# Zero products in the mixer of a two-layer block: seven, one and one at the start of each layer in place of eight spread over it

## The reference

```python
for l in range(DEPTH):
    x = layer_norm(ALPHA * x + 0.5 * swiglu(x, ffn_w1[l, 0], ffn_w2[l, 0]), ...)
    mix = hybrid_mixer(x, w_in[l], ...)
    x = layer_norm(ALPHA * x + mix, ...)
    x = layer_norm(ALPHA * x + 0.5 * swiglu(x, ffn_w1[l, 1], ffn_w2[l, 1]), ...)

def hybrid_mixer(x, ...):
    proj = x @ w_in                                  # 1024 x 7168
    b_gate, c_gate, v, x_r, y_r, g_logits = split(proj)
    y_a = (b_gate * causal_depthwise_conv(c_gate * v, sc_w, 3)) @ w_out_conv
    xc = causal_depthwise_conv(x_r, rc_w, 4) + rc_b
    gates = sigmoid(per-head 256x256 products of xc + rg_b)
    h = rg_lru(xc, gates[0], gates[1], a_param)      # a scan over the tokens
    y_b = (h * gelu(y_r)) @ w_out_rnn
    g_a, g_b = split(sigmoid(g_logits + b_merge))
    return (g_a * y_a + g_b * y_b) @ w_o
```

## Time and profile before

| | |
|---|---|
| median of three runs | 1782.72 us (1781.75 to 1782.98) |
| the profiled execution | 1781.71 us, its span 1780.0 us |
| TensorE products (PE) | 1750.6 us busy, 98% of the span, 10818 products |
| TensorE weight loads (PEld) | 1543.8 us, 87% |
| VectorE (DVE) | 1372.5 us, 77% |
| ScalarE (ACT) | 988.6 us, 56% |
| chain that ended last | PE 81%, DVE 10%, ACT 3% |
| 256-column products of `cols_unit` (L2295 to L2297) | 912 of each line, 254.0 us each |
| mean granted clock of TensorE | 0.997 |

### The profile page before, as it was taken

One profiled execution on the slowest core, in us unless ns is written; L12 is line 12 of the kernel. 1 busy time (PEld: TensorE's weight loads), 2 busy tenths in 40 slices (PEclk: granted clock), 3 DMA queues, 4 the chain that ended last, 5 costly groups with the idle time before them and its releaser, 6 DMA issues.

```text
span 1780.0 us, 27901 instructions
## 1 busy us (share of the span) xinstructions
PE 1750.6 (98%) x10818; PEld 1543.8 (87%) x10818; DVE 1372.5 (77%) x1544; ACT 988.6 (56%) x973; POOL 60.9 (3%) x103
## 2 busy tenths in 40 slices
PE   9999999999999999999999999999999989999998
PEld 8888899998888878888999988888899868777776
DVE  7656886857778875567878667788878888889988
ACT  5555465643544545445656435445544636879984
POOL 2000000000000000000000000000200010000002
PEclk9999999999999999999999999999999999999999
DMA  7555455564577645554555645777454029989994
GB/s 267 202 174 207 173 188 188 190 252 150 198 274 283 260 168 184 191 200 179 177 202 181 246 166 173 280 283 274 139 175 143 24 91 339 385 301 412 426 376 159
DMA packets 58487, 395.21 MB, mean 222 GB/s; under 512 B 7216, under 2 KB 7616, under 8 KB 12816
## 3 DMA queue, kind: packets, MB, share of 16 engines
q1 hardware_dynamic: 48800, 350.31, 53.7%
q0 software_dynamic: 9568, 43.44, 7.2%
q10 hardware_dynamic: 16, 0.01, 0.0%
HBM read 386.37 MB, written 7.36 MB: 221 GB/s over the span
## 4 chain that ended last, share of the span: by engine, by line
PE 81%; DVE 10%; ACT 3%; DVEq 3%; issue 3%; ACTq 0%
PE ps L2304 18%; PE ps L2312 9%; PE ps L2296 8%; PE ps L2297 8%; PE ps L2295 8%; PE ps L2502 3%; PE ps L2501 3%; PE ps L2505 3%; DVE wlo L1844 3%; PE ps L1035 2%; DVE wlo L2810 2%; PE ps L1037 2%; PE ps L1036 2%; PE ps L1099 1%; ACT whi L1344 1%
## 5 line engine op out<-in xcount | busy, mean ns | idle before, releaser
L2810 DVE TENSOR_TENSOR wlo<-raw,whi 128x2048 fp32r<-128x2048 f32 x235 | 536.5, 2289 | 238.4 <-ACT whi L2635 236.4
L2635 ACT ACTIVATE whi<-raw 128x2048 fp32r<-128x2048 f32 x235 | 449.2, 1912 | 375.3 <-PE ps L2505 170.7
L2304 PE MATMUL ps<-xT,whi 128*128 128x512 f32 x1408 | 340.0, 393 | 2.6 <-DVE xT L2829 2.2
L2304 PEld LDWEIGHTS ps<-xT,whi 128*128 128x128 f32 x1408 | 262.4, 188 | 60.4 <-DVE xT L2829 3.0
L2295 PE MATMUL ps<-xT,whi 128*128 128x256 f32 x912 | 254.0, 278 | 0.3 <-DVE wlo L2810 0.3
L2297 PE MATMUL ps<-xT,wlo 128*128 128x256 f32 x912 | 254.0, 279 | 0.0
L2296 PE MATMUL ps<-xT,whi 128*128 128x256 f32 x912 | 254.0, 279 | 0.0
L2312 PEld LDWEIGHTS ps<-xT,wlo 128*128 128x128 f32 x1408 | 174.1, 188 | 7.8
L2312 PE MATMUL ps<-xT,wlo 128*128 128x256 f32 x1408 | 175.5, 277 | 0.0
L2296 PEld LDWEIGHTS ps<-xT,whi 128*128 128x128 f32 x912 | 171.3, 188 | 0.6
L2295 PEld LDWEIGHTS ps<-xT,whi 128*128 128x128 f32 x912 | 171.1, 188 | 0.5 <-DVE wlo L2810 0.5
(11 more groups left out here) (616 smaller groups left out, 3204.0 us busy)
## 6 DMA issues: line engine op xcount, KB each, us to landing
raw<-stream SPq DMA_DIRECT2D x236, 1024.0 KB, 4.9
raw<-experts SPq DMA_DIRECT2D x64, 1024.0 KB, 7.6
mod<-experts SPq DMA_DIRECT2D x32, 1024.0 KB, 7.3
adaraw<-ada POOLq DMA_DIRECT2D x24, 1024.0 KB, 5.1
yd<-lnrow POOLq DMA_DIRECT2D x7, 512.0 KB, 7.8
lnrow<-ln_g POOLq DMA_DIRECT2D x6, 512.0 KB, 4.9
lnrow<-ln_b POOLq DMA_DIRECT2D x6, 512.0 KB, 6.7
yd<-lnrow POOLq DMA_DIRECT2D x10, 256.0 KB, 6.5
```

Of the source, the lines that this page charges most:

```text
L2304: last = nc.tensor.matmul(bank(b), whi[:, slot, c:c + P], xT[:, k].rearrange("p a t -> p (a t)"), start=k == 0, stop=False)
L2635: act_fn(whi[:, slot, :], raw[:, slot, :], ACT.Copy).then_inc(hi_done, 1)
L2810: v.tensor_tensor(wlo[:, slot, :], raw[:, slot, :], whi[:, slot, :].bitcast(F32), ALU.subtract).then_inc(lo_done, 1)
```

## The change

The leads of the second half, of u6 and u11 of the first half, and of the conv and rnn units go. In the first half of each layer u1 gets seven leads in a row, u2 one and u3 one. That is nine leads in a layer, where there were eight.

```diff
-LED_UNITS = (1, 6, 11)
+LED_UNITS = {1: 7, 2: 1, 3: 1}
...
                 weights_ready(rnd, slot)
                 if lead is not None:
-                    nc.tensor.matmul(bank(lead), zero_w[:, :], whi[:, slot, 0:512], start=True, stop=True)
+                    b, count = lead
+                    for _ in range(count):
+                        nc.tensor.matmul(bank(b), zero_w[:, :], whi[:, slot, 0:512], start=True, stop=True)
...
-                                cols_unit(rnd, slot, xThi, xTlo, [bank(b, 0, T), bank(b, T)], b if u in LED_UNITS else None)
+                                cols_unit(rnd, slot, xThi, xTlo, [bank(b, 0, T), bank(b, T)],
+                                          (b, LED_UNITS[u]) if hf == 0 and u in LED_UNITS else None)
...
-                        cols_unit(*at(base, i), yahi, yalo, [bank(q, 0, T), bank(q, T)], q if q == 0 else None)
+                        cols_unit(*at(base, i), yahi, yalo, [bank(q, 0, T), bank(q, T)])
...
-                        cols_unit(*at(base, i), ybhi, yblo, [bank(q, 0, T), bank(q, T)], q if q == 0 else None)
+                        cols_unit(*at(base, i), ybhi, yblo, [bank(q, 0, T), bank(q, T)])
```

## The result

| | before | changed |
|---|---|---|
| median, seven executions each, one comparison | 1782.72 us (1781.75 to 1784.50) | 1789.96 us (1786.30 to 1790.96) |
| the profiled execution | 1781.71 us | 1790.06 us |
| its mean granted clock | 0.997 | 0.995 |

The ratio is 1.0036, 95% interval 1.0025 to 1.0046: slower, by some 7 us, where 9.6 us less were forecast.

The account below looks back on a forecast made before the run. TensorE, never idle, bounds the mixer. Fast units win 10.0 us, leads cost 0.4 us: 9.6 us off the profiled 1781.71 us gives 1772.1 us, plus 1.0 us for the median 1773.1 us; whole range 1771.5 to 1787.7 us.

Parts of the forecast that it names:

- What bounds the mixer: Mixer: TensorE busy throughout (27.20 of 27.20 us), its products are the path; units take 5.440 or 5.653 us, changing at leads.
- The leads' price: Mixer: sixteen leads go (3.8 us), eighteen come (4.2 us), seven in a row costing 1.63 us; net 0.4 us more.
- The place behind seven leads: Ahead of u1: seven leads forget their beginning and leave one slow place; 70 of 74 units fast, 10.0 us won; chance 0.50.
- slow-one: Mixer stream's place one lead after fast: 5.653 us a unit, with two more leads needed to make it fast.
- The seven settle in another place: Ahead of u1: seven end in fast or slow-two, leaving 2 fast units of 74; 4.9 us more, 1787.6 us; chance 0.28.
- No lead comes after, so u3 to the last rnn unit, 35 units a layer, stay fast: Mixer from u3 on: the fast pace lasts without leads, 70 of 74 units fast; 47 units at 0.213 us, 10.0 us won.
- what hides the rest: Mixer: VectorE's splits may come late once u6 to u10 are fast; 20 units stay slow, 4.3 us given back, 1777.4 us.
- 23 of 74: Mixer units from u1 to the last rnn unit that are fast before the change: 14 in layer 0, 9 in layer 1.
- Mere counting: Ahead of u1: seven leads act as one; 36 fast units, 2.8 us won, 0.4 us paid, 1780.3 us; chance 0.19.
- slow-two: Mixer stream's place one lead after slow-one: slow pace, 5.653 us a unit, and the next lead makes fast.
- The pace is not the leads' doing: Mixer: leads do not set the pace, only two more leads count; 0.4 us more, 1783.1 us; chance 0.03.

Follow-up runs that it names:

- the first map: The changed kernel with single leads and groups of 2 to 8 and 16 ahead of every unit of `cols_unit` in both layers; 1813.78 us.

## Why the prediction was wrong

*What bounds the mixer*: right. TensorE has no pause in the changed mixers; the paces are 5.44 and 5.65 us a unit in every run, nothing between but where a unit meets a wait; leads move the place.

*The leads' price*: right. Seven 1.62 us (1.63 forecast, ends 1.58 and 1.82), nine in a layer 2.1 us.

*The place behind seven leads*: the step that failed. "So I read seven leads as a run that forgets its beginning and ends in slow-one." They do end in slow-one out of fast and out of slow-two; out of slow-one, where u0 stands in the changed kernel, they end in a fourth place. The step took three things for granted. That a run of six has settled on one distance and forgets: the table shows none that forgets, and leads out of fast do not settle (the starts of the first map's seven out of fast are 237 and 230 ns apart in turn, up to the sixth). That sixteen products of the feed-forward part speak for zero products ahead of a unit: sixteen of these do otherwise. And that the places are the three that the trace of before shows; that trace holds single leads, and single leads never enter the fourth. The rival "The seven settle in another place" said what follows, with its price of 4.9 us; that its two remaining fast units are lost too makes it 5.3 us, which the windows confirm. The median is 7.2 us above that of before. The other 1.9 us can come from executions of before with 28 fast units in place of 23 (1.1 us) and from the clock in the second block; how the two share it is not shown.

*"No lead comes after, so u3 to the last rnn unit, 35 units a layer, stay fast"*: would have failed as well. The pace lasts without a lead (37 units in the run with none), but not through a wait, and a fast stream makes one: after ten fast units at ScalarE's read ahead of the second half, after fifteen at VectorE's split for u11 of the second half. With the place right, u3 to u14 would by my estimate at most have been fast: 24 units against 23, and nothing won. The part on what hides the rest named late splits as a loss of 4.3 us for units that go back to the slow pace while the wait lasts; it did not see that behind one wait of 0.13 us all units of the layer run slow. That no run shows u3 to u14 fast with the changed kernel's own leads is because its start never allowed it.

*"23 of 74"*: one execution's count. Another has 28, five units or 1.1 us more to lose.

*Mere counting*: falls. Seven counted as one lead make slow-two out of slow-one, and the lead ahead of u2 then makes fast; u2 is slow in both layers.

*The pace is not the leads' doing*: falls too; only the 0.4 us of two more leads would be left, and the mixers lost 5.3 us. The Trainium skill, "TensorE: Matmul & The Clock Gate", section "Back-to-back issue gap", gives an isolated product one gap by its column count alone, and says that in a stream the weight loads share in setting it. One gap for one column count disagrees with every run here that shows both 113.3 and 117.8 ns for 256 columns.

## What to carry to other kernels

Where an engine's pace depends on a state, what an operation does to the state has to be seen from every state, in the very stream where it will stand; a law read from single steps did not extend to runs of them. A state that is never restored is only as good as its start and as the first wait behind it: look for what resets it before multiplying a gain per unit by all the units that follow, and spread the steps if the start is not fixed, as the eight leads of the kernel before do, which made 23 and 28 of 74 units fast from the starts seen. And before a bounding engine is made faster over a long stretch, read the cover of every operand and buffer along it, not only of those known to be late.

## What the runs showed of the hardware that was not expected

The fourth place, at 117.8 ns a product; groups of three to eight zero products out of it or out of fast, which in every case seen end in slow-one for an odd count and in the fourth place for an even one; a delay of 0.13 us, ahead of which a stream runs at 113.3 ns a product and behind which the 570 products left run at about 118; and equal instructions of u0 that leave TensorE in one of four places, not the same from execution to execution.
